# Second output projection cut into two halves along its inner dimension, and four groups of tiles moved to other SBUF addresses

## The reference, cut to what matters

```python
h_ml  = mlstm_chunkwise(...)                 # 4 heads x 128 = 512 columns
h_mla = causal_block_attention(q, k, v)      # 8 heads x 64  = 512 columns
mix = jnp.concatenate([h_ml, h_mla], axis=-1) @ w_out      # (512 x 1024) @ (1024 x 1024)
x = x + rmsnorm(mix, norm_post_mix)
y = jnp.square(jax.nn.relu(m @ w_up)) @ w_down             # m = rmsnorm(x), 4096 hidden
```

## Time and profile before

| | us |
|---|---|
| median of 3 timed executions | 1473.61 (1472.83 to 1474.70) |
| the profiled execution, its own time | 1473.68 |
| span of that execution in the trace | 1471.9 |
| TensorE busy | 1376.7 (94%) |
| VectorE busy | 636.5 (43%) |
| ScalarE busy | 521.5 (35%) |
| GpSimd busy | 521.9 (35%) |

### The profile page before, as it was taken

The page is one execution under the profiler, slowest core; times in us unless marked ns, Lnnn a source line. Parts: engine busy times, 40 slices in busy tenths (PEclk is TensorE's granted clock), DMA queues, the critical chain, the costliest instruction groups (busy, mean ns, idle before and its releaser), DMA issues.

```text
span 1471.9 us, 15715 instructions
## 1 busy us (share of the span) xinstructions
PE 1376.7 (94%) x6273; PEld 1088.5 (74%) x6273; DVE 636.5 (43%) x848; ACT 521.5 (35%) x794; POOL 521.9 (35%) x229
## 2 busy tenths in 40 slices
PE   4899989999999999999997998977979999999997
PEld 3677889867888888888775865544848888888885
DVE  6557866256213531121365535455155532414223
ACT  4467111354322221221344434544234322313232
POOL 2233250233544544443441332200314444444441
PEclk7899999999999999999998999989989999999998
DMA  5222210122333333332331331100213333333321
GB/s 165 58 71 58 58 30 15 44 86 86 107 92 96 99 100 88 99 100 78 109 96 29 91 70 45 43 15 1 72 43 86 94 92 101 99 88 101 96 76 57
DMA packets 215457, 111.66 MB, mean 76 GB/s; under 512 B 16141, under 2 KB 213593, under 8 KB 215385
## 3 DMA queue, kind: packets, MB, share of 16 engines
q1 hardware_dynamic: 214584, 109.81, 26.3%
q10 hardware_dynamic: 672, 0.79, 0.2%
q0 software_dynamic: 128, 0.07, 0.0%
HBM read 108.55 MB, written 2.10 MB: 75 GB/s over the span
## 4 chain that ended last, share of the span: by engine, by line
PE 86%; DVE 9%; ACT 3%; issue 1%; POOL 1%; DMA 0%; DVEq 0%; ACTq 0%; SPq 0%
PE bank L1674 22%; PE bank L1676 22%; PE bank L1675 22%; PE aux L1849 2%; PE aux L1048 1%; PE aux L1862 1%; PE bank L1697 1%; PE bank L1698 1%; PE bank L1699 1%; PE aux L1859 1%; PE bank L1033 1%; DVE al L2209 1%; PE aux L962 1%; PE aux L974 1%; DVE rstd L2217 1%
## 5 line engine op out<-in xcount | busy, mean ns | idle before, releaser
L1636 POOL TENSOR_TENSOR wl<-raw,wh 128x1024 fp32r<-128x1024 f32 (+1 forms) x202 | 499.5, 2475 | 886.3 <-ACT wh L1953 886.0
L1674 PE MATMUL bank<-ah,wh 128*128 128x512 f32 x1016 | 404.2, 398 | 0.1
L1675 PE MATMUL bank<-ah,wl 128*128 128x512 f32 x1016 | 397.1, 391 | 0.0
L1676 PE MATMUL bank<-al,wh 128*128 128x512 f32 x1016 | 397.0, 391 | 0.0
L1953 ACT CAST wh<-raw 128x1024 fp32r<-128x1024 f32 (+1 forms) x202 | 209.4, 1039 | 386.2 <-PE bank L1676 372.0
L1674 PEld LDWEIGHTS bank<-ah,wh 128*128 128x128 f32 x1016 | 191.7, 189 | 44.8 <-issue 5.3
L1676 PEld LDWEIGHTS bank<-al,wh 128*128 128x128 f32 x1016 | 191.6, 189 | 40.6
L1675 PEld LDWEIGHTS bank<-ah,wl 128*128 128x128 f32 x1016 | 191.7, 189 | 40.0 <-issue 1.4
L1674 PE MATMUL bank<-yh,wh 128*128 128x512 f32 x432 | 171.2, 396 | 0.0
L1676 PE MATMUL bank<-yl,wh 128*128 128x512 f32 x432 | 170.6, 395 | 0.0
L1675 PE MATMUL bank<-yh,wl 128*128 128x512 f32 x432 | 170.6, 395 | 0.0
(11 more groups left out here) (378 smaller groups left out, 1616.5 us busy)
## 6 DMA issues: line engine op xcount, KB each, us to landing
raw<-in_w_up SPq DMA_DIRECT2D x54, 512.0 KB, 4.0
raw<-in_w_down SPq DMA_DIRECT2D x48, 512.0 KB, 4.1
raw<-in_w_in SPq DMA_DIRECT2D x40, 512.0 KB, 3.9
raw<-in_w_gate SPq DMA_DIRECT2D x22, 512.0 KB, 3.8
raw<-in_w_out SPq DMA_DIRECT2D x16, 512.0 KB, 4.2
raw<-in_ple_gate SPq DMA_DIRECT2D x8, 512.0 KB, 4.0
raw<-in_w_down SPq DMA_DIRECT2D x8, 384.0 KB, 3.4
xtok<-in_x SPq DMA_DIRECT2D x4, 512.0 KB, 5.0
```

Of the source, the lines that this page charges most:

```text
L1636: nc.gpsimd.tensor_tensor(wl[b % SPLIT][:, 0:w], raw[b % RAW][:, 0:w], wh[b % SPLIT][:, 0:w].bitcast(F32), ALU.subtract).then_inc(wl_ready, 1)
L1674: nc.tensor.matmul(ps, h[:, c:c + P], mh[:, k, :], start=(n == 0), stop=False)
L1675: nc.tensor.matmul(ps, l[:, c:c + P], mh[:, k, :], start=False, stop=False)
L1676: last = nc.tensor.matmul(ps, h[:, c:c + P], ml[:, k, :], start=False, stop=(n == nk - 1))
```

## The change

1. `wout2` becomes two kinds of tiles. `wouta` multiplies slices 0 to 3 (the first 512 rows of `w_out_2`), `woutb` slices 4 to 7. Each has 4 blocks of 512 rows by 256 columns, so a block serves two tiles; the number of blocks (8) and of matmuls (96 and 96 for 192) is the same.
2. TensorE computes `wouta` tile m into `aux[0]`, one PSUM bank outside the ring of four, in the attention loop: behind `attention(i)` nothing at ib = 0, slice 0 at ib = 1, slice 1 at ib = 2, slices 2 and 3 at ib = 3. So 3, 3 and 6 matmuls follow the steps of a head, and tile m belongs to head m.
3. VectorE copies `wouta` tile m out of `aux[0]` into `part2` at step i = 4 (m + 1), the last one behind the loop and behind the last `lower`. For `woutb` it adds the bank and `part2` into `acc`, where it copied before.
4. ScalarE calls `tile("wouta", m)` at steps i = 5, 9, ..., 29 and once behind the loop; where a block's predecessor is finished this does the next cast.
5. `yh`/`yl`, `ph`/`plo` and `cqh`/`cql`/`ckh`/`ckl` are placed a multiple of 256 bytes from `wh0`. Everything that stands behind them in the same layout moves along.

```diff
-    wide("wout2", "w_out_2", 0, 8)
+    for half, kind in enumerate(("wouta", "woutb")):
+        for j in range(4):
+            blocks.append(("mat", "w_out_2", half * 4 * P, 4, j * 256, 256))
+            for i in range(2):
+                tiles.append((kind, 2 * j + i, len(blocks) - 1, i * P, 4, 256))
...
+        def in_step():
+            top[0] += (offs["wh0"] - top[0]) % 256
         top[0] = free
+        in_step()
         yh = [sb(f"yh{i}", [P, KD, T], F32R) for i in range(2)]
...
         ptok = sb("ptok", [P, NC, 2 * P])
+        in_step()
         ph = sb("ph", [P, 2, T], F32R)
...
         rtmp = sb("rtmp", [P, T])
+        in_step()
         cqh = sb("cqh", [P, 2, T], F32R)
...
+        part2 = sb("part2", [P, KD, T], at=offs["og"])
...
+            def first_half(m, k):
+                if m == 0 and k == 0:
+                    pe.wait_ge(al_ready, KD * F_MIX2 + 4)
+                    pe.wait_ge(ml_rn, H)
+                gemm("wouta", m, part=(k, 4), into=aux[0])
             for i in range(NI):
                 attention(i)
+                for k in ((), (0,), (1,), (2, 3))[i % NC]:
+                    first_half(i // NC, k)
             att_values(MLA_H - 1)
             pe.wait_ge(pt_evac, NI)
             pe.wait_ge(prob_ready, NI)
-            pe.wait_ge(al_ready, KD * F_MIX2 + 7)
+            late = (ah[:, 4:KD, :], al[:, 4:KD, :])
             for m in range(KD - 1):
-                gemm("wout2", m, ready=(al_ready, KD * F_MIX2) if m == 0 else None)
-            gemm("wout2", KD - 1, part=(0, 2))
+                gemm("woutb", m, mov=late, ready=(al_ready, KD * F_MIX2 + 4) if m == 0 else None)
+            gemm("woutb", KD - 1, mov=late, part=(0, 2))
             ssq(4, early=True)
-            gemm("wout2", KD - 1, part=(1, 2))
+            gemm("woutb", KD - 1, mov=late, part=(1, 2))
...
+                if i > NC and i % NC == 1:
+                    tile("wouta", i // NC - 1)
             upper(F_MIX2, 7, 7, pv[1][:, :], (pv_ps, MLA_H))
+            tile("wouta", KD - 1)
...
+            def first_half(m):
+                ps = tile("wouta", m, aux[0])
+                if m == 0:
+                    dve.wait_ge(nd_ps, 4 * H)
+                    dve.wait_ge(h32_ready, H32_BASE[F_MIX2] + H)
+                freed(nc.vector.tensor_copy(part2[:, m, :], ps))
...
+                if i > 0 and i % NC == 0:
+                    first_half(i // NC - 1)
             lower(F_MIX2, 7, 7, pv[1][:, :])
+            first_half(KD - 1)
             for m in range(KD):
-                ps = tile("wout2", m)
-                freed(nc.vector.tensor_copy(acc[:, m, :], ps))
+                ps = tile("woutb", m)
+                evacuated(dve, "wouta", m)
+                freed(nc.vector.tensor_tensor(acc[:, m, :], ps, part2[:, m, :], ALU.add))
```

More of the change, by code:

```diff
@@ L178 @@
                   gate="act", up="dve", down="dve", proj="act", pgate="act", gates2="dve", qk2="act", v2="act",
-                  cq2="act", ckv2="act", o2="act", uq2="dve", uk2="act", uv2="dve", wout2="dve",
+                  cq2="act", ckv2="act", o2="act", uq2="dve", uk2="act", uv2="dve", wouta="dve",
+                  woutb="dve",
                   up2="act", down2="dve")
@@ L563, in build @@
         LAST_USE = {F_NORM1: pl.done("z", 3), F_MIX1: pl.done("wout", 7), F_NORM2: pl.done("up", (2, 5)),
-                    F_PLE: pl.done("pgate", 7), F_NORM3: pl.done("o2", 3), F_MIX2: pl.done("wout2", 7),
+                    F_PLE: pl.done("pgate", 7), F_NORM3: pl.done("o2", 3), F_MIX2: pl.done("woutb", 7),
                     F_NORM5: pl.done("up2", (3, 7))}
@@ L1294, in scalar_second @@
                     upper(F_MIX2, 4 + t, 4 + t, pv[t % 2][:, :], (pv_ps, 2 * t + 2))
+                if i > NC and i % NC == 1:
+                    tile("wouta", i // NC - 1)
             upper(F_MIX2, 7, 7, pv[1][:, :], (pv_ps, MLA_H))
+            tile("wouta", KD - 1)
             for m in range(KD):
                 if m > 0:
-                    evacuated(act, "wout2", m - 1)
+                    evacuated(act, "woutb", m - 1)
                     square(4, m - 1, acc[:, m - 1, :])
-                tile("wout2", m)
-            evacuated(act, "wout2", KD - 1)
+                tile("woutb", m)
+            evacuated(act, "woutb", KD - 1)
             square(4, KD - 1, acc[:, KD - 1, :])
@@ L1547, in add_normed @@
                     nc.vector.tensor_tensor(x[:, k, :], x[:, k, :], h32[:, k % 3, :], ALU.add).then_inc(done, 1)
-            evacuated(dve, "wout2", KD - 1)
+            evacuated(dve, "woutb", KD - 1)
             dve.wait_ge(al_ready, KD * (F_MIX2 + 1))
@@ L1649, in _, with gemm @@
             state = dict(t=0)
-            def gemm(kind, idx, mov=None, ready=None, order=None, part=None):
+            def gemm(kind, idx, mov=None, ready=None, order=None, part=None, into=None):
                 t = state["t"]
@@ L1658, in gemm @@
                 if t >= NBANK:
-                    eng, n = pl.read[t - NBANK]
+                    eng, n = pl.read[t - (NBANK if into is None else 1)]
                     pe.wait_ge(bank_read[eng], n)
@@ L1663, in gemm @@
                 h, l = wh[b % SPLIT], wl[b % SPLIT]
-                ps = bank[t % NBANK][:, :]
+                ps = (bank[t % NBANK] if into is None else into)[:, :]
                 if part and part[0] < part[1] - 1:
@@ L2191, in link, with tile @@
                 dve.wait_ge(dve_step, count[0])
-            def tile(kind, idx):
+            def tile(kind, idx, ps=None):
                 while pl.READER[pl.tiles[tnow[0]][0]] != "dve":
@@ L2200, in tile @@
                 dve.wait_ge(gemm_done, t + 1)
-                return bank[t % NBANK][:, :]
+                return (bank[t % NBANK] if ps is None else ps)[:, :]
             def freed(i):
```

## The result

The changed kernel takes 1456.19 us (median of 4 executions, 1454.50 to 1457.06) against 1473.22 for the kernel before: ratio 0.9886, 95% interval 0.9872 to 0.9900. That is 17 us less; 17.6 were forecast. The profiled execution took 1455.51 us with a span of 1453.7, against 1473.68 and 1471.9.

What follows compares the result with a forecast made beforehand. TensorE, busy for 94% of the span, was taken as the bound. The terms -9.0 - 21.7 + 12.1 (loop) + 0.6 + 0.4 gave -17.6 us, from 1473.68 to 1456.1 us; own range 1452 to 1460, wide range 1452 to 1465.5.

Steps and rivals of the forecast that it cites:

- Addresses: Gemms with displaced activations: 1392 matmuls each 6.6 ns quicker once placed at multiples of 256 bytes, 9.0 us saved.
- Projection: Behind the attention loop: 96 of 192 matmuls leave that stretch, 21.7 us less.
- early sum: Behind the loop: the early sum waits 0.4 us for tile 5's square to be added.
- Heads 1, 3, 5: Attention loop: 2.72 us of inserted matmuls fill a 0.81 us gap, so each head grows by 1.91 us.
- Heads 2, 4, 6: Attention loop: 0.48 us of a 1.83 us gap stays, so each head grows by 1.37 us.
- Head 0: First head of the loop: TensorE is busy, the clock rises at the same moment as before, growth 2.72 us.
- Last head: End of the loop: inserted matmuls use gaps and the values run at full clock, so it shrinks by 1.2 us.
- Seams: Loop: changes between fp32r and f32 matmuls around the insertions cost 0.1 us a head, 0.8 us in all.
- Casts: Loop: three ScalarE casts make the scores of the third step 0.2 us late each, 0.6 us in all.
- held scalings: Loop: GpSimd's 2.41 us holds VectorE's scaling until 5.5 us after the head's start; cost 0, at worst 7.2 us.
- slower than before: Rival, heads 1 to 7: the clock stays at 1.2 GHz, costing 8.9 us per head so spent; chance 0.03.
- The loop grows by all it takes: Rival, heads 0 to 6: gaps move instead of closing, growth 19.0 us, not 12.5, ending at 1462.6; chance 0.12.

Runs made afterwards that it cites:

- the shift of everything: The changed kernel with every SBUF tile moved up by 128 bytes, distances kept: 1454.72 us, ratio 0.9877 against the kernel before.
- the variant with two slices first: The changed kernel with slices 0 and 1 behind each head's second step, slice 2 behind the third, slice 3 behind the fourth: 1452.98 us, ratio 0.9877.

## Why the prediction was right, step by step

- **Addresses, 9.0 us.** Right in kind and size: 8.5 us in the two traces (4.0 and 4.7, less 0.2 that the traces differ by before any `yh` is used), 9.8 alone, 7.9 as the last part added. The 6.6 ns a matmul, for which the rows shown give 7.0, and the 1296 matmuls on `yh`/`yl` held; the 12 on `ckh`/`ckl` were left out of the count, less than 0.1 us. The doubt that "far" might be the cause was settled by the changed kernel itself and by the shift of everything: only distances count. The Trainium skill ("SBUF — State Buffer", section "SBUF: two separate sides") would have had no cost here; displaced `yh`, and displaced weights in the run with `wl` moved, show one of 2.2 to 7.5 ns a matmul.
- **Projection, -21.7, and early sum, +0.4.** 21.3 less in the traces, 21.3 forecast. The early sum waited 0.23 us, not 0.4.
- **Heads 1, 3, 5: +1.91 each.** 8.88 - 6.98 = 1.90. **Heads 2, 4, 6: +1.37 each, and 0.2 for casts.** 9.44 - 8.00 = 1.44.
- **Head 0: +2.72.** 10.34 - 9.12 = 1.2 in the traces. This is a term that was mis-sized: the prediction let the clock rise at the same moment, and it rose sooner. The trace of before has a granted clock of 0.61 from 970 to 978, which is 6.2 us at half speed and the rest at full speed, so the rise came some 6 us after the head's start (the prediction read 7); the one after has 0.60 from 966 to 970 and 1.00 from 970 to 978, a rise after some 3 us:

```profile
966.00:970.00 4.00, 3.99 (x16) 3.35 (x17) 2.75 (x8) 1.76 (x6) 0.00 (x0) 0.60 0.00 0
970.00:978.00 8.00, 8.00 (x40) 5.01 (x39) 4.27 (x13) 3.08 (x11) 0.00 (x0) 1.00 0.00 0
```

  The three kernels with nothing in head 0 took 9.12, 9.01 and 7.55 us there, the last (new addresses alone) with the early rise; the ten traces with 12 matmuls spread over it took 10.2 to 10.5, all with the early rise. So its growth is 1.2 to 2.8 us. The early rise can come without the inserted matmuls, but came in one trace of three without them and in ten of ten with them: whether they bring it about is open.
- **Last head: -1.2.** 6.57 against 7.50, -0.93. The values ran at the upper clock, as forecast (0.66 to 1.00 granted). But the kernel with new addresses alone, with nothing inserted, was at the upper clock there too and took 5.92 us. So the shrinking is all clock: at an equal clock the last head too grows, by 0.65 us.
- **Seams, +0.8.** The odd heads' totals leave no room for any, and yet the seams are there. From start to start, the three inserted matmuls lengthen the way from x2 to x3 by 0.75 us (1.30 below, 0.55 before), the six that from x4 to x1 by 1.38 (2.58 for 1.20 us), where pace alone gives 0.68 and 1.36:

```profile
994.67 0.44 PE L1075 MATMUL aux<-cst,pm 128*128 128x128 f32 x2
...
995.97 0.49 PE L1075 MATMUL bank<-cst,pm 128*128 128x128 f32 x3
...
997.54 0.60 PE L1075 MATMUL aux<-cst,pm 128*128 128x128 f32 x4
...
1000.12 0.27 PE L1075 MATMUL bank<-cst,pm 128*128 128x128 f32 x1
```

  With 0.07 us for the way from x3 to x4 the seams come to an estimated 0.17 us a head. The gap was longer than forecast by as much: 0.81 us counts from a modelled end. The mask's matmul at 980.43 could have been followed 0.05 us after its start, as the one of the next head is (below), so TensorE stood still for 0.98 us. Two misreadings cancelled; that is luck.

```profile
986.58 0.22 PE L1035 MATMUL bank<-mask,ident 128*128 128x128 bf16 x1
986.63 0.50 PE L1062 MATMUL bank<-cst,pm 128*128 128x128 f32 x3
```

- **Casts, +0.6, and held scalings.** The scores behind the x4 came at once (989.10 behind transposes begun at 988.61); the 0.6 was not there. The held scaling was: in the changed kernel it ran from 989.15 for 1.70 us, and ended at 990.85, as GpSimd's subtraction ended at 990.77.

```profile
988.26 2.51 POOL L1673 TENSOR_TENSOR wl<-raw,wh 128x1024 fp32r<-128x1024 f32 x1 [29.15 <-ACT wh L1990]
...
989.15 1.70 DVE L1516 TENSOR_SCALAR pm<-pm,am 128x128 f32<-128x128 f32 x1
...
991.25 0.27 PE L1075 MATMUL bank<-cst,pm 128*128 128x128 f32 x1
```

  Forecast: held to 5.5 us after the head's start, wanted at 5.9. Seen: 990.77 - 985.23 = 5.5, and 991.25 - 985.23 = 6.0. It cost nothing by 0.4 us. In the variant with two slices first TensorE was there 5.5 us after the head's start (989.62 + 0.23 - 984.39), 0.5 us sooner, and it did cost. The rule of the exclusive pair (the Trainium skill, same page and section) holds in each of these.

The loop's total was 10.3 for 12.1 and 0.6 forecast; that 2.4 is head 0's clock (1.5), the seams (0.8, which the longer gaps paid for) and the casts (0.6), less 0.5 in the other heads. It was offset by 1.4 us in the second MLP's start and behind the last matmul, which no step of the prediction touched, and by 0.5 us less from the addresses. So the mechanism was right, but that the total came so close (17.0 us by the medians, 18.2 by the traces, for 17.6) is in part luck: terms of 1 to 2 us cancelled. Against the kernel with new addresses alone, whose loop of 58.4 us had the clock's early rise and no fall at its end, the loop grew by 13.5 us, not 10.3.

The rival "slower than before" didn't come: all heads from 1 on ran at the upper clock. "The loop grows by all it takes" didn't either: heads 1 to 6 grew by 1.4 to 1.9 us, not 2.7.

## What to carry to other kernels

Read the pace of back-to-back matmuls from the differences of their starts, tile by tile: 6.6 ns each is invisible in a busy share and is 9 us in 1400 of them. For matmuls like these, keep all operands a multiple of 256 bytes apart, weights and both halves included; for others, measure it first. Before moving work into a loop bound by a chain, list each gap with what ends it and what stands before it: the work is free up to the gap that lies behind it and costs its full length beyond, and helpers that come along (here a cast and a subtraction) are placed by the same list.

## What was not expected of the hardware

- The distance between the operands of matmuls, modulo 256 bytes, costs, and their addresses do not (226.7 ns for both placements of everything; 233.3 for activations displaced by 32, 96, 128, 192 or 224 bytes, 234.2 by 160, 228.9 by 64).
- A displaced weight tile slows two intervals of three (231.1 ns on average).
- One layout can run at two paces within one execution: 228.9 and 233.3 ns with al alone displaced. What tips it is open.
- The clock's rise behind the same idle stretch came 3 to 6 us after TensorE was busy again (3.2 and 6.2 us in the traces of after and before). Where the stretch was filled, it had not fallen. That moves the time of single executions by 1 to 3 us; of two kernels 1 us apart the heads told more than the medians.
